# Block two of a two-block transformer: the first chunk of each layer, and what TensorE does in two waits

## The reference, cut to what matters

```
h = x @ w_in                                  # 1024 x 5704 columns: dq dk dv sq sk sv iq ik iw ga gb
ya = diff_attention(dq, dk, dv)               # causal, 4 heads of two maps
yb = dsa_attention(sq, sk, sv, iq, ik, iw)    # index scores iq . ik choose 64 keys a query
x  = layer_norm(ALPHA * x + (sigmoid(ga) * (ya @ w_bd) + sigmoid(gb) * (yb @ w_bs)) @ w_o)
ffn = hierarchical_moe(x)                     # 32 experts of 1024 x 256, two of them a token
ple = sigmoid(x @ w_ple_gate) * (p @ w_ple)
x  = layer_norm(ALPHA * x + ffn + ple)
```

## Time and profile before

| | |
|---|---|
| Time, median of 3 runs (lowest to highest) | 1842.4 us (1838.01 to 1848.89) |
| The profiled execution's own time | 1839.58 us |
| Its span | 1837.8 us |
| Mean granted clock of PE | 0.953 |
| PE, DVE, ACT, POOL busy | 1621.5, 1095.0, 746.2, 4.7 us |
| Mixers of layer 0, from its first product | about 873 to 1117 us |
| Experts of layer 0 | about 1117 to 1345 us |
| Mixers of layer 1 | about 1358 to 1600 us |
| Experts of layer 1 and the last norm | about 1600 to 1834 us |

### The profile page before, as it was taken

One profiled execution on the slowest core, in us unless ns is written; L12 is line 12 of the kernel. 1 busy time (PEld: TensorE's weight loads), 2 busy tenths in 40 slices (PEclk: granted clock), 3 DMA queues, 4 the chain that ended last, 5 costly groups with the idle time before them and its releaser, 6 DMA issues.

```text
span 1837.8 us, 25972 instructions
## 1 busy us (share of the span) xinstructions
PE 1621.5 (88%) x10438; PEld 1277.2 (69%) x10438; DVE 1095.0 (60%) x1541; ACT 746.2 (41%) x972; POOL 4.7 (0%) x5
## 2 busy tenths in 40 slices
PE   6999989997999989995999899868669999997774
PEld 6877789996877779995887676534358777753432
DVE  5966767787876768775478572222165976512124
ACT  3566545553556545552445642101034664311111
POOL 0000000000000000000000000000000000000000
PEclk9999999998999999998899999989889999998988
DMA  6543355544552535552644298999955436999995
GB/s 229 183 156 125 126 183 183 196 147 157 189 183 92 172 130 193 182 204 69 204 149 146 89 414 346 413 423 414 412 160 173 135 118 239 366 417 419 417 419 226
DMA packets 174258, 422.56 MB, mean 230 GB/s; under 512 B 15969, under 2 KB 68553, under 8 KB 157513
## 3 DMA queue, kind: packets, MB, share of 16 engines
q1 hardware_dynamic: 174152, 421.07, 62.4%
HBM read 419.99 MB, written 1.05 MB: 229 GB/s over the span
## 4 chain that ended last, share of the span: by engine, by line
PE 25%; DMA 17%; DVE 6%; issue 2%; ACT 2%; SPq 1%; DVEq 0%
PE lot L308 5%; PE lot L310 5%; PE lot L309 5%; DMA raw<-w_exp_up 4%; PE lot L2200 4%; DMA two_e_gates<-w_exp_up 3%; DMA two_e_sqT<-w_exp_up 3%; DMA e_lo<-w_exp_up 3%; DMA e_hi<-w_exp_down 3%; PE lot L2269 1%; DMA raw<-w_out 1%; SPq L2097 1%; PE lot L2170 1%; DVE w_lo L267 1%; PE lot L2227 1%
## 5 line engine op out<-in xcount | busy, mean ns | idle before, releaser
L267 DVE TENSOR_TENSOR w_lo<-raw,w_hi 128x2048 fp32r<-128x2048 f32 (+3 forms) x195 | 433.8, 2230 | 150.3 <-ACT w_hi L262 149.6
L262 ACT ACTIVATE w_hi<-raw 128x2048 fp32r<-128x2048 f32 (+3 forms) x196 | 364.9, 1867 | 150.2 <-PE lot L310 132.5
L308 PE MATMUL lot<-one_hT_hi,w_hi 128*128 128x256 f32 x704 | 201.1, 286 | 5.5 <-DVE one_hT_lo L415 5.5
L309 PE MATMUL lot<-one_hT_lo,w_hi 128*128 128x256 f32 x704 | 200.8, 285 | 0.0
L310 PE MATMUL lot<-one_hT_hi,w_lo 128*128 128x256 f32 x704 | 200.8, 285 | 0.0
L308 PE MATMUL lot<-w_hi,two_hT_hi 128*128 128x512 f32 (+1 forms) x448 | 182.4, 407 | 9.9 <-DVE w_lo L267 8.6
L310 PE MATMUL lot<-w_hi,two_hT_lo 128*128 128x512 f32 (+1 forms) x448 | 177.3, 396 | 0.0
L309 PE MATMUL lot<-w_lo,two_hT_hi 128*128 128x512 f32 (+1 forms) x448 | 177.2, 396 | 0.0
L308 PE MATMUL lot<-w_hi,one_hT_hi 128*128 128x512 f32 (+2 forms) x384 | 149.5, 389 | 5.6 <-DVE w_lo L267 2.9
L310 PE MATMUL lot<-w_hi,one_hT_lo 128*128 128x512 f32 (+2 forms) x384 | 145.8, 380 | 0.0
L309 PE MATMUL lot<-w_lo,one_hT_hi 128*128 128x512 f32 (+2 forms) x384 | 145.6, 379 | 0.0
(11 more groups left out here) (441 smaller groups left out, 3173.0 us busy)
## 6 DMA issues: line engine op xcount, KB each, us to landing
raw<-w_in SPq DMA_DIRECT2D x78, 1024.0 KB, 5.1
raw<-ffn_w_up SPq DMA_DIRECT2D x44, 1024.0 KB, 5.2
raw<-ffn_w_down SPq DMA_DIRECT2D x22, 1024.0 KB, 5.0
raw<-w_out SPq DMA_DIRECT2D x16, 1024.0 KB, 6.0
raw<-w_exp_gate SPq DMA_DIRECT2D x14, 1024.0 KB, 18.1
raw<-w_exp_up SPq DMA_DIRECT2D x14, 1024.0 KB, 21.0
two_e_gates<-w_exp_up SPq DMA_DIRECT2D x12, 1024.0 KB, 19.2
e_lo<-w_exp_up SPq DMA_DIRECT2D x10, 1024.0 KB, 21.9
```

The costliest lines, as they stand in the source:

```text
L262: act.activation(K.hi[:, r, 0:n], self.raw(name)[:, 0:n], ACT.Copy).then_inc(K.sig["hi_ready"], 1)
L267: dve.tensor_tensor(K.lo[:, r, 0:n], self.raw(name)[:, 0:n], K.hi[:, r, 0:n].bitcast(F32), ALU.subtract).then_inc(K.sig["lo_ready"], 1)
L308: pe.matmul(out, a[0], b[0], start=start, stop=False)
L309: pe.matmul(out, a[0], b[1], start=False, stop=False)
```

## The change

1. The first chunks are ordered ik, iq0, iq1 instead of iq0, iq1, ik. So ik takes raw buffer 0, and iq0 and iq1 the two buffers that the last expert chunks free late. The small loads that hung behind ik hang behind iq1, the last of the three as before.
2. PE multiplies tile 0 by ik before it transposes tile 1; ik and iq parts are then interleaved, and the last before dq are 24 wide matmuls of iq1.
3. No subtraction is on POOL. DVE subtracts ik between the norms of tile 0 and tile 1, and iq0 after the norm of tile 1 and ahead of `tile_lo` of tile 1.
4. `dq1` is subtracted after the rotation of the index columns instead of before it.
5. `warm` transposes the identity into an unused PSUM corner: 36 times at the start of layer 1's list, and 44 times in each layer between `down(6)` and `hidden(7, half 1)`.
6. `overflow` is read earlier on PE, ACT and DVE: ahead of `down(6)`, of the copy of its result and of the subtraction.
7. `turn(7)` stands between tile 0's and tile 1's parts of `give(6)`.

```diff
+LAST_TURNS = 44
+SEAM_TURNS = 36
-TWO_CHUNKS = ["iq0", "iq1", "ik", "dq0", "dq1", "dk0", "dk1", "sq0", "sq1", "sk0", "sk1", "dv0", "dv1", "sv0", "sv1",
+TWO_CHUNKS = ["ik", "iq0", "iq1", "dq0", "dq1", "dk0", "dk1", "sq0", "sq1", "sk0", "sk1", "dv0", "dv1", "sv0", "sv1",
+    def warm(self, pe, turns):
+        for _ in range(turns):
+            pe.transpose(self.K.ps[3][:, 0, 256:384], self.K.ident[:, :], self.K.ident[:, :])
...
-    ST = Stream(K, L, TWO_CHUNKS, TWO_WIDTHS, TWO_ENDS, {}, FFN_TURN, {}, by_pool=("iq0",) if before else (),
+    ST = Stream(K, L, TWO_CHUNKS, TWO_WIDTHS, TWO_ENDS, {}, FFN_TURN, {}, by_pool=(),
-    first_slot = {"iq0": 0, "iq1": 1, "ik": 2}
+    first_slot = {"ik": 0, "iq0": 1, "iq1": 2}
...
+        if before:
+            E.warm(pe, SEAM_TURNS)
+        transpose_tile(K, L, pe, K.x, "xTt0", 0, x_normed)
+        L.claim(pe, "ik")
+        L.claim(pe, "iq")
+        both("xTt0")
+        first_part("ik", 0)
+        transpose_tile(K, L, pe, K.x, "xTt1", 1, x_normed)
+        first_part("iq", 0, 0, 2)
+        both("xTt1")
+        first_part("ik", 1)
+        first_part("iq", 1, 0, 2)
+        first_part("iq", 0, 1, 2)
+        first_part("iq", 1, 1, 2)
...
             if q == NQ - 2:
+                more_rounds = E.overflow(pe)
                 E.down(pe, q, 0)
+                E.warm(pe, LAST_TURNS)
             E.hidden(pe, q + 1, 0, 1)
...
-        more_rounds = E.overflow(pe)
-        E.give(pe, NQ - 2)
+        E.give(pe, NQ - 2, tiles=(0,))
         E.turn(pe, NQ - 1, 0)
+        E.give(pe, NQ - 2, tiles=(1,))
...
-            tile_lo(dve, 1)
-        else:
-            ST.lo_to(dve, "iq1")
-            tile_lo(dve, 1)
-        ST.lo_to(dve, "iq0", 2)
-        ST.lo_to(dve, "iq1", 2)
+            ST.lo_to(dve, "iq0")
+        tile_lo(dve, 1)
+        ST.lo_to(dve, "iq1", 1)
         ST.lo_to(dve, "ik", 2)
...
         norm_dve_of(K, dve, link, "n2", 0, M.ln_g, M.ln_b)
+        if stage.after:
+            stage.after.ST.lo_to(dve, "ik")
```

More of the change, by code:

```diff
@@ L2232, in down, with give @@
             last.then_inc(K.sig["e_half"], 1)
-    def give(self, pe, q, i=None):
+    def give(self, pe, q, i=None, tiles=range(T)):
         self.drained(pe, f"W{q}", i)
         self.drained(pe, f"Y{q}.0", i)
-        for t in range(T):
+        for t in tiles:
             for n in range(2):
@@ L2910, in scalar @@
             tile_hi(act, 0)
-            tile_hi(act, 1)
-            ST.hi_to(act, "iq0", 1)
-        else:
-            tile_hi(act, 1)
-        first_hi(act, "ik")
+            ST.hi_to(act, "iq0")
+        tile_hi(act, 1)
+        first_hi(act, "iq1")
         columns("iq")
@@ L3055, in scalar @@
         if stage.after:
-            stage.after.first_hi(act, "iq0")
+            stage.after.first_hi(act, "ik")
         act.activation(st[:, 232:233], K.ident[:, 0:1], ACT.Sqrt)
@@ L3059, in scalar @@
         if stage.after:
-            stage.after.first_hi(act, "iq1")
+            stage.after.first_hi(act, "iq0")
             stage.after.tile_hi(act, 0)
@@ L3359, in vector @@
             else:
+                more_rounds = E.overflow(dve)
                 E.out_lo(dve, q, 0)
```

34 lines of the change are left out of this document (11 added, 23 removed).

## The result

The changed kernel takes 1834.45 us in the median of 8 runs (1830.64 to 1838.16), the kernel before 1844.88 us (8 runs, 1838.01 to 1848.89). The ratio is 0.9948, with a 95% interval of 0.9931 to 0.9964: faster by half a per cent, 10.4 us by the medians. The forecast was 1829 us, from a sum of 12 us.

A forecast was written before the change was run, and what follows sets the result against it. Expert streams were taken as DMA-bound and projections as PE-bound, with the change in four short places neither covers. Terms summed to -12.0 us: 1827.6 from the profiled execution, 1830.4 from the median, forecast 1829 us, range 1823 to 1838.

The forecast's parts named there:

- Layer 0's start: Layer 0's first products: smaller ik lands and is split sooner, dq starts at the high clock; -2.5 us.
- 44 transposes, layer 0: Layer 0's last quarter: transposes during the weight wait keep the clock high, matmuls take 3.65 instead of 6.22; -2.6 us.
- `turn(7)` and the flag, layer 0: Layer 0's last quarter: flag load and turn no longer delay `down(7)`, which starts at 1333.6, not 1334.94; -1.35 us.
- The seam with dq's clock: Between the layers: earlier norm without POOL, ik first, dq starting at the high clock; -3.0 us, between -2.4 and -6.4.
- 44 transposes, layer 1: Layer 1's last quarter: matmuls fall from 5.35 to 3.65 us, less 0.2 us of delay; -1.5 us.
- `turn(7)` and the flag, layer 1: Layer 1's last quarter: same reordering, where the flag cost 0.21 us; -1.1 us.
- rival 1: Both last quarters: the transposes do not hold the clock; 1833.3 us, chance 0.12.
- rival 2: Layer 0's start and seam: gains do not travel because DVE sets the attention behind them; 1834.5 us, chance 0.14.
- The 0.2 us that layer 1's turns were to be late: Layer 1's last quarter: 44 transposes end at 1806.7, 0.2 us behind the waiting matmuls' start at 1806.50.
- dq's first 4 us: Sign expected in the profile behind the index and query products: clock 1.00 in dq's first 4 us.
- rival 3: Last quarters: transposes run at the low clock, 0.24 us each, and delay the matmuls; 1844 us, chance 0.05.
- tile 0's narrow products would run mostly at the low clock: Seam: after a 3.8 us gap on PE, ik's 24 narrow products take 0.22 us each, 5.2 us.

The follow-up runs named there:

- chunks: Changed kernel without any warming transposes and with quarter 6 and the overflow test as before; 1836.64 us, 0.9969 of the kernel before.
- early: Changed kernel with the seam's 36 transposes moved ahead of the branch over the overflow rounds; 1832.98 us, 0.9941 of the kernel before.
- seam0: Changed kernel without its 36 transposes at the seam; 1833.09 us, 0.9938 of the kernel before.
- again: Changed kernel measured once more, nothing edited; 1833.03 us, 0.9937 of the kernel before.
- last0: Changed kernel without the 44 transposes behind `down(6)`; 1838.29 us, 0.9969 of the kernel before.
- last22: early_fill with 22 transposes in place of 44 in the last quarters; 1831.09 us, 0.9929 of the kernel before.
- early_fill: early with 28 more transposes between tile 0's transposes and its narrow products; 1828.45 us, 0.9918 of the kernel before.

## Why the prediction was right, and where it was not

The time, 1834.45, lay 5.45 us above the forecast and inside the range of 1823 to 1838 that the prediction works out; the mechanism was the one named, but for the seam. Step by step, each term against its stretch (changed minus before):

| Step | Forecast | Measured |
|---|---|---|
| Layer 0's start | -2.5 | -2.6 |
| 44 transposes, layer 0 | -2.6 | -2.6 (6.22 to 3.66) |
| `turn(7)` and the flag, layer 0 | -1.35 | -1.26 (4.65 to 3.39) |
| The seam with dq's clock | -3.0 | +0.6 - 1.8 = -1.2 |
| 44 transposes, layer 1 | -1.5 | -1.7 (5.35 to 3.66) |
| `turn(7)` and the flag, layer 1 | -1.1 | -1.1 (the rest of 31.28 - 28.51 = 2.77) |
| Sum | -12.0 | -10.4 (-10.4 by the medians too) |

**Right.** The transposes hold the clock (rival 1 falls: 3.66 us and 1.00 behind them, in both layers). The page of the Trainium skill that the forecast weighed, "TensorE: Matmul & The Clock Gate", Part 4, is contradicted by these rows, if `pe.transpose` is what it calls transpose mode; the trace has these transposes as MATMUL and does not say. The gains of the front travelled (rival 2 falls): layer 0's start is 2.6 us shorter up to the end of top-k, and chunks shows the same in the whole time, -5.7 for -5.5 in the stretches. The 0.2 us that layer 1's turns were to be late did not come: they ended 1.3 us ahead of the weights, since PE's wait there was 6.3 us and not the 4.6 of the trace that the forecast read; twelve of the fourteen traces have it at 6.3 in layer 1. `down(7)` stands 1326.10 - 1324.11 = 2.0 us behind `product`, forecast 1.9. dq's first 4 us have the clock of 1.00.

**Mis-sized: the seam.** The step that failed is the seam's term of -3.0, in the sentence "PE has been free since 1344.26, so its 36 transposes (3.9 us) end at 1348.2, ahead of tile 0's norm at 1349.0". On the new scale they should have ended 3.9 us behind the last product and ended 10.5 us behind it. Two things were missing. The branch over the overflow rounds stands between the last product and the turns, and PE has nothing for 3.46 us there; in the kernel before this lay inside 6.76 us of waiting for the norm, so no row showed it. By the traces a fetch of 16 KB of instructions lies in it (early, above). And by the end of that idle time the clock had gone, so that the turns cost 0.2 us apiece, which is the mechanism of rival 3 at the place where I had not put it. early shows both: ahead of the branch, no idle time and 4.09 us. The forecast that tile 0's narrow products would run mostly at the low clock was wrong for the changed kernel (its late turns did warm them: 2.3 us at 1.00) and right for seam0 and early. All this cost the seam 1.8 us against the forecast: seam0 gives back 1.3 us.

**Mis-sized: the level.** The terms together account for 1.6 of the 5.45 us (-12.0 and -10.4). The other part, 3.9, is the time that the sum was taken from. The forecast was put between the profiled execution's 1839.6 and the median of three runs, 1842.4. With 8 to 25 runs that median is 1843.6 to 1844.9, above the 1841 that 1829 + 12 stands for. The profiled execution was a lucky one: its mixer took 141.0 us, the least of fourteen traces. This is also why the two profiles seem to say that 4 us of the gain were lost in layer 1's mixer (141.0 to 145.0): the traces do not bear that out. The five of the old order average 144.0 us there and the nine of the new order 144.7, and the sum of the other stretches, -10.4, is the whole difference of the medians; with 4 us lost the gain would be 6.4 us, outside the interval of the changed kernel (6.6 to 12.7 us) and far outside that of again (9.2 to 13.8).

**A slip.** The prediction's wide product, 10.1 / 43, is 0.235 us and not 0.233; over its 36 wide products that is under 0.1 us.

**Left open.** The 3.46 us are 1.0 us until the fetch starts, 1.0 of fetch and 1.4 until PE's first turn; what PE does in the first and the last of these, and why the first is 0.3 us in last0, no run shows. Nor is the cover by early turns whole in every trace: in last22 tile 0's transposes start 0.9 us later behind the last product than in early_fill, with VectorE's norm at its usual place. There the fetch started 2.8 us behind the last product, at 1342.82, where early_fill has it 1.3 behind, at 1341.22. It ended at 1344.03, and the transposes came 1.6 us behind it, at 1345.63. What delayed the fetch is open.
